# Row block 1's norm ahead of the low parts of the third quarter in the shared layer-norm routine of a two-block transformer kernel

## What is computed

```python
for i in range(DEPTH):                      # DEPTH = 2
    h = mixer_a(x, ...) if i < N_A_LAYERS else mixer_b(x, ...)
    x = layer_norm(ALPHA * x + h, ln_g[i], ln_b[i])
    x = x + (p[i] @ w_ple[i]) * sigmoid(x @ w_ple_gate[i])
...
h = _rmsnorm(x, pre_mix_g) * (1.0 + scale_a) + shift_a
proj = h @ w_in
```

## Time and profile before

| | |
|---|---|
| median of 3 runs | 2229.97 us (2229.56 to 2232.17) |
| the profiled execution | 2231.24 us, of which the span is 2229.4 us |
| TensorE busy | 98% of the span |
| VectorE, ScalarE, GpSimd busy | 65%, 45%, 0% |
| mean granted TensorE clock | 0.995 of full |
| read from HBM | 493.52 MB, 223 GB/s over the span |

### The profile page before, as it was taken

One profiled execution on the slowest core, in us unless ns is written; L12 is line 12 of the kernel. 1 busy time (PEld: TensorE's weight loads), 2 busy tenths in 40 slices (PEclk: granted clock), 3 DMA queues, 4 the chain that ended last, 5 costly groups with the idle time before them and its releaser, 6 DMA issues.

```text
span 2229.4 us, 24586 instructions
## 1 busy us (share of the span) xinstructions
PE 2181.2 (98%) x10387; PEld 1811.5 (81%) x10387; DVE 1442.8 (65%) x1420; ACT 1011.1 (45%) x996; POOL 6.5 (0%) x17
## 2 busy tenths in 40 slices
PE   8999999999999999999999999989999999999998
PEld 8878888777888788777888988867888888888887
DVE  5778667775755777767966775487545544544656
ACT  5443563433436633434454566544434434443442
POOL 0000000000000000000000000000000000000000
PEclk9999999999999999999999999999999999999999
DMA  8867649475966466758853325365556656655753
GB/s 287 309 242 270 240 151 388 179 287 193 371 255 238 170 246 268 277 211 329 338 179 104 122 93 196 118 236 213 203 190 231 224 186 215 244 185 199 266 179 125
DMA packets 73310, 499.36 MB, mean 224 GB/s; under 512 B 8945, under 2 KB 9457, under 8 KB 16369
## 3 DMA queue, kind: packets, MB, share of 16 engines
q1 hardware_dynamic: 72784, 497.66, 61.5%
q10 hardware_dynamic: 416, 0.13, 0.0%
HBM read 493.52 MB, written 4.24 MB: 223 GB/s over the span
## 4 chain that ended last, share of the span: by engine, by line
PE 93%; DVE 5%; ACT 2%; issue 1%; DMA 0%; ACTq 0%; DVEq 0%; SPq 0%
PE products L2336 68%; PE products L2347 14%; PE aside L2653 1%; PE transposed L2772 1%; PE transposed L2410 1%; DVE w_low L1422 1%; ACT w_high L839 1%; PE transposed L2500 1%; PE aside L2500 1%; PE transposed L2468 1%; DVE x_low L1538 0%; PE products L2759 0%; PE aside L2759 0%; PE aside L2940 0%; PE transposed L2930 0%
## 5 line engine op out<-in xcount | busy, mean ns | idle before, releaser
L1422 DVE TENSOR_TENSOR w_low<-raw,w_high 128x2048 fp32r<-128x2048 f32 (+3 forms) x336 | 744.2, 2218 | 566.1 <-ACT w_high L839 565.0
L839 ACT ACTIVATE w_high<-raw 128x2048 fp32r<-128x2048 f32 (+3 forms) x336 | 622.4, 1855 | 821.2 <-PE products L2336 668.3
L2336 PE MATMUL products<-w_high,x_high 128*128 128x512 f32 (+2 forms) x1688 | 651.2, 386 | 12.3 <-DVE w_low L1422 9.7
L2336 PE MATMUL products<-w_high,x_low 128*128 128x512 f32 (+2 forms) x1688 | 644.0, 382 | 0.0
L2336 PE MATMUL products<-w_low,x_high 128*128 128x512 f32 (+2 forms) x1688 | 643.6, 381 | 0.0
L2336 PEld LDWEIGHTS products<-w_high,x_high 128*128 128x128 f32 x1688 | 318.2, 189 | 73.3 <-issue 14.2
L2336 PEld LDWEIGHTS products<-w_high,x_low 128*128 128x128 f32 x1688 | 318.2, 188 | 60.1
L2336 PEld LDWEIGHTS products<-w_low,x_high 128*128 128x128 f32 x1688 | 318.4, 189 | 59.4 <-issue 1.4
L1436 DVE SCALAR_TENSOR_TENSOR raw<-raw,cond_row 128x2048 f32<-128x2048 f32 x96 | 220.2, 2294 | 0.4 <-DMA raw<-in_w_mod 0.3
L2347 PE MATMUL products<-w_high,x_high 128*128 128x512 f32 (+1 forms) x472 | 192.7, 408 | 11.4 <-DVE w_low L1422 5.9
L2336 PE MATMUL products<-w_high,u_high 128*128 128x512 f32 x496 | 193.7, 391 | 0.0
(11 more groups left out here) (439 smaller groups left out, 1898.6 us busy)
## 6 DMA issues: line engine op xcount, KB each, us to landing
raw<-in_w_mlp SPq DMA_DIRECT2D x128, 1024.0 KB, 4.9
raw<-in_w_mod SPq DMA_DIRECT2D x96, 1024.0 KB, 5.2
raw<-in_w_ple SPq DMA_DIRECT2D x32, 1024.0 KB, 7.0
raw<-in_w_a_qkv SPq DMA_DIRECT2D x24, 1024.0 KB, 6.2
raw<-in_w_b_kvq SPq DMA_DIRECT2D x24, 1024.0 KB, 7.3
raw<-in_w_a_gate SPq DMA_DIRECT2D x16, 1024.0 KB, 5.7
raw<-in_w_a_out SPq DMA_DIRECT2D x16, 1024.0 KB, 7.1
raw<-in_w_b_gate SPq DMA_DIRECT2D x16, 1024.0 KB, 5.7
```

The lines of the kernel that those rows point to most:

```text
L839: act.activation(split_tile(m, 0, st, u, j, 0, n), m.raw[:, RAW_SLOT[at], 0:n], ACT.Copy).then_inc(m.s_w_high, 1)
L1422: dve.tensor_tensor(lo, m.raw[:, RAW_SLOT[at], 0:n], hi.bitcast(F32), ALU.subtract).then_inc(m.s_raw_used, 1)
L2336: ins = pe.matmul(bank, x[:, x0 + kk, a], w, start=first and kk == 0 and n == 0, stop=last and kk == st.kq - 1 and n == 2)
```

## The change

In ScalarE's `rows_in` the square root for row block 1 moves ahead of the x_high copy of item 2, and the x_high copy of item 3 ahead of the high part of the fourth quarter. In VectorE's `rows_in` `whole(1)` moves ahead of the low part of the third quarter and of x_low 2, and x_low 3 moves ahead of the norm of row block 1's chunk 1. TensorE's, SyncE's and GpSimd's programs stay as they are, and no instruction is added or removed.

```diff
@@ scalar_program, rows_in
         high_unit(name, 0, [2])
         if between:
             between()
-        row_high(ROWS_THREE, [2])
+        std(1, 2)
+        row_high(ROWS_THREE, [2, 3])
         high_unit(name, 0, [3])
-        std(1, 2)
-        row_high(ROWS_THREE, range(3, 8))
+        row_high(ROWS_THREE, range(4, 8))
@@ vector_program, rows_in
         normalise(0, 2)
         row_low(ROWS_THREE, 1)
+        whole(1)
         low_unit(following, 0, [2])
         row_low(ROWS_THREE, 2)
-        whole(1)
+        row_low(ROWS_THREE, 3)
         normalise(1, 1)
-        row_low(ROWS_THREE, 3)
         normalise(1, 2)
         row_low(ROWS_THREE, 4)
```

## The result

The changed kernel takes 2237.1 us in the median (2236.5 to 2240.12, 6 runs) against 2230.6 us for the kernel before (2229.56 to 2232.17, 6 runs): a ratio of 1.0033, 95% interval 1.0022 to 1.0043. It is **slower by 6.5 us**, 0.3%; the forecast was 6.0 us slower (2236.0) and a range of 2233.4 to 2239.0. The profiled execution has a span of 2235.8 us, 6.4 more than before.

What follows compares the result with a forecast made beforehand. TensorE, busy 98% of the span, bounds the kernel, so only its standing still or lower clock counts. Terms 1.50 + 1.50 + 3.05 = 6.05 us over the median 2229.97 gave 2236.0 us, range 2233.4 to 2239.0.

Steps and rivals of the forecast that it cites:

- Place 1 and 2: Calls of the changed routine for `ple0` and `ple1`: half three 1.33 us late awaiting x_low 2, +1.45 each.
- The term for the norm of (1,1): Each place: this norm, now behind x_low 3, delays item 4's transposes by 0.05 us, up to 0.2 allowed.
- Place 3: Call for `c_f`: half three waits 4.30 us more for x_low 2; +3.0 in sum with equal clock.
- The wait for the normed chunk: In `c_f`, item 3's transposes no longer wait for row block 1's first normed chunk: -1.37 us.
- The clock term: In `c_f`, one low-clock stretch of 1.52 us replaces that of before: 0, bounds -1.5 and +1.5.
- E: Rival: in `c_f` the 1.37 us wait and 1.52 low stretch go, nothing else moves: 2227.1 us, chance 0.04.
- C: Rival: the clock holds in `c_f`: 2234.5 us, chance 0.14.
- D: Rival: slack later than `c_f` takes its delay back, 3.0 us less: 2233.0 us, chance 0.10.
- B: Rival: clock falls also in `ple0` and `ple1`, or twice in `c_f`, 1.5 us per stretch: 2239.0, chance 0.12.

Runs made afterwards that it cites:

- run 1: Kernel before with only x_low 3 ahead of the norm of (1,1) and x_high 3 ahead of quarter four's high part; `whole(1)` unmoved: 2230.47 us, ratio 0.9998.
- run 2: Changed kernel, but the norm of (1,1) stays ahead of x_low 3: 2237.79 us, ratio 1.0033 to the kernel before.
- run 3: Kernel before with the new order for `ple0` and `ple1` alone, `c_f` keeping the old order: 2233.53 us, ratio 1.0012.
- run 8: Kernel before, no edit, traced once more: 2230.06 us, one execution.
- run 9: Kernel before, no edit, traced yet another time: 2231.2 us, one execution.
- run 6: Kernel before with one other exchange, x_low 6 ahead of the norm of chunk (1,3): 2227.85 us, ratio 0.9989.
- run 7: run 6 with TensorE's transposes of item 3 one step sooner in half three: 2228.25 us, ratio 0.9987 to the kernel before.
- run 10: Changed kernel, no edit, traced once more: 2238.87 us, one execution.
- run 4: Kernel before with the new order for `c_f` alone: 2234.66 us, ratio 1.0021.
- run 5: Changed kernel, but quarter three's low part goes ahead of `whole(1)`, only x_low 2 staying behind it: 2236.94 us, ratio 1.0028 to the kernel before.
- run 11: Changed kernel with TensorE's transposes of item 3 moved from half three's last step to half two's: 2234.11 us, ratio 1.0014 to the kernel before.

## Why the prediction was right, and which term was not

The mechanism was right and the total came close; the closeness of the total is in part luck, since one term, the clock in place 3, was too small.

**Place 1 and 2: right to the term.** Half three 1.33 us late (1.33 measured), transposes of item 4 1.45 late (1.45), the 0.71 behind it untouched, VectorE idle for 3.50 where about 3 were foretold. The term for the norm of (1,1), which the change puts just ahead of item 4's transposes, was 0.05 with up to 0.2 allowed; the transposes took 0.63 instead of 0.60, and nothing more is seen. Runs 1 and 2 show no price of the exchange around x_low 3. Places 1 and 2 alone cost 2.7 us in run 3, against 3.0 in the sum.

**Place 3: the waits were right.** Half three's delay was put at 4.30; from half one to half three it is 10.26 in the changed kernel (989.00 to 999.26) and 6.01 before (986.20 to 992.21), so 4.25. The wait for the normed chunk went, as foretold, and bought back its 1.4.

**The clock term was mis-sized.** The step "one low stretch at the price of before, 1.52 for 1.52, that is 0" took the one execution at hand for the rule. Over the executions traced:

| order in place 3 | length of place 3, us | slow stretch |
|---|---|---|
| old: before, runs 8 and 9, runs 1 and 3 | 31.21; 29.71, 29.69; 29.71, 29.69 | 1 of 5 |
| old with x_low 6 sooner: run 6 | 29.02 | 0 of 1 |
| the same with the transposes sooner, one wait of 1.89 us: run 7 | 29.03 | 0 of 1 |
| new: after, runs 10, 2, 4 | 33.89; 34.94, 34.28, 34.00 | 4 of 4 |
| new with w_low first, a wait of 3.27 us: run 5 | 33.23 | 1 of 1 |
| new with the transposes in half two, waits of 1.96 and 0.53 us: run 11 | 33.14 | 1 of 1 |

Waits of 1.2 and 0.7 us left the clock up in five of the six executions that had them (in runs 1, 3, 6, 8 and 9, not in the first of before); 4.1 us at once brought it down in four of four. Between them it is open: one wait of 1.89 us left it up in run 7, one of 1.96 us had it down at the resumption in run 11. The four of the new order have a mean of 34.28, 4.6 above 29.7. So the usual price of place 3 is 4.2 to 5.2 us, not 3.05, of which some 3 are the waits and 1.2 to 2.3 the clock. By the medians it is 3.8 (run 4, with an interval of 2.7 to 6.7). The bound of +1.5 on the clock term covered most of it; the value taken did not. With 4.6 for place 3 the sum would have been about 7.6 us, against 6.5 measured (interval 4.9 to 9.6), so the forecast's 0.5 us of closeness says nothing for its clock term; it lies within the spread of the medians, about 1 us.

The trace of before held a warning that the prediction did not use. Its idle stretch nearest to 4.3 us is neither of the two in the earlier trace rows but one of 5.18 us, and the low clock behind it lasted past 1498, longer than the low stretch of 3.37 us in place 3 whose price was taken (the second row is the stretch behind that wait, with a granted clock of 0.50):

```profile
1491.13 1.11 PE L2468 MATMUL transposed<-const,mix 128*128 128x128 f32 x4 [5.18 <-DVE mix L2217]
...
1491.13:1498.00 6.87, 5.18 (x16) 3.84 (x17) 6.84 (x7) 2.16 (x4) 0.00 (x0) 0.50 0.46 153
```

**The rivals.** E (faster by 2.9) asked for x_low 2 by 992.21; in both traces of the changed kernel it ended more than 4 us later than that point. Its remark on place 1, that x_low 2 would be pushed by 3.2 us, should read 3.1 (415.28 to 418.35), which changes nothing. C (the clock holds) is excluded by the four executions of the new order. D (later slack takes the delay back) did not happen: the shift of 5.48 behind place 3 is 6.18 near 1190 and 6.4 at the end. B's fall of the clock in places 1 and 2 appears in none of the executions: two waits of 1.16 and 0.71 us with more than 3 us of work between them left the clock at 1.00 in each of them. B's other half, two stretches in place 3, is near what run 10 shows (2.3 us where B had 3.0). The rule that the prediction takes from the Trainium skill (TensorE: Matmul & The Clock Gate, "What's actually happening"), that the gate throttles after idling, agrees with this case's traces in that the wait of 4.1 us in place 3 was followed by a stretch at 1.2 GHz each time. That 1.2 and 0.7 us, broken by work, were followed by one only once in six executions is what the runs add.

**The 0.7 us in `c_hq`** were in nobody's sum. The wait of 0.3 to 0.9 us near 1100 is in the changed kernel's first trace, in runs 2, 7, 8 and 9, and not in the other eight; the kernel before has it in two of three traces. It comes and goes with the execution. The low part that TensorE then awaits starts 10.8 us after an earlier one that had waited for ScalarE's high part, and ScalarE had waited for the transfer of that quarter. In the five traces with the wait the awaited low part starts 79.9 to 80.8 us behind the end of place 3, in the other eight 78.4 to 79.7. What makes the transfer late in one execution and not in another stays open.

## What to carry to other kernels

Before moving work ahead in an engine's queue, ask for which instruction the slowest engine next waits, and what the moved work stands in front of. VectorE had 1.8 us in hand ahead of half three in place 1 and was pushed back by 3.1 there, for a chunk that TensorE's own order did not take up until 5 us later. In this kernel the earlier chunk was used only once TensorE's order was changed with it, and even then it just made good the loss in places 1 and 2 (run 11). The cheap exchanges are found the other way round, from the standing waits: run 6 took one away by letting a 0.6 us low part pass a norm of 1.4 us that nobody waited for. A slow stretch in a single profile is a sample, so trace a kernel more than once before entering such a stretch on either side of a sum.

## What was not expected of the hardware

The same two short waits in TensorE's work (1.2 and 0.7 us) were followed by a stretch at 1.2 GHz in one execution and not in five others with TensorE's order unchanged. A single wait of about 1.9 us went either way (run 7: clock up; run 11: down at the resumption). After 4.1 us of standing still the clock fell in all four executions, but not at the same time: in one about 1.1 us after TensorE had resumed, in another before it did, and the stretch cost 1.2 us in the first (5.41 against 4.19) and 2.3 in the second (6.48).
